# Fillers of 32 and 992 bytes in the place of 64 and 960 around the normalised input: it begins at 160 modulo 2048 in a partition

## What is computed

```python
for l in range(DEPTH):                      # 2
    h = rmsnorm(x, norm_mix[l])
    p = h @ w_in[l]                         # 2048 x 4608
    ...                                     # differential attention (q, k, v), pooling mixer, convolution mixer
    x = x + concat([y_b, y_a, y_c]) @ w_out[l]      # 2048 x 2048
    h = rmsnorm(x, norm_ffn[l])
    gu = h @ w_ffn_in[l]                    # 2048 x 11008
    g = causal_dwconv(gu[..., :D_FF], ffn_conv_w[l], ffn_conv_b[l])
    x = x + (silu(g) * gu[..., D_FF:]) @ w_ffn_out[l]   # 5504 x 2048
return rmsnorm(x, final_norm)
```

## The kernel before, in words

| tile | bytes | begins at, modulo 2048 |
|---|---|---|
| `x` | 16384 | 128 |
| `xg` (and over it, for the end of layer 1, `xt`, `gains`, `ss`, `rt`) | 32768 | 192 |
| `ssq` | 1024 | 192 |
| `raw`, `whi`, `wlo` | 16384 each | 128 |
| `half`, `gt` | 4096, 4128 | 1184 |
| `y` | 4096 | 1216 |
| `hidden1` | 88064 | 128 |
| `mix`, `hidden0`, `qT` | 32768, 88064, 8192 | 192 |
| `pw_sb` | 8192 | 672 |

## Time and profile before

### The profile page before, as it was taken

One profiled execution on the slowest core, in us unless ns is written; L12 is line 12 of the kernel. 1 busy time (PEld: TensorE's weight loads), 2 busy tenths in 40 slices (PEclk: granted clock), 3 DMA queues, 4 the chain that ended last, 5 costly groups with the idle time before them and its releaser, 6 DMA issues.

```text
span 2082.2 us, 32567 instructions
## 1 busy us (share of the span) xinstructions
PE 2065.1 (99%) x11564; PEld 1792.5 (86%) x11564; DVE 1418.0 (68%) x2009; ACT 1081.7 (52%) x1509; POOL 23.5 (1%) x20
## 2 busy tenths in 40 slices
PE   9999999999999999999999999999999999999998
PEld 8888888888888888888888888888888888888886
DVE  7998777676666665555489978676666666654454
ACT  6556655555555554433374566455555555544444
POOL 0001100000000000000000011000000000000000
PEclk9999999999999999999999999999999999999999
DMA  8554354555555555555565444555555555555554
GB/s 290 176 186 158 129 191 178 206 188 191 189 189 185 198 192 190 195 194 180 207 209 198 176 147 137 198 191 190 191 190 181 200 186 195 185 212 192 194 200 162
DMA packets 108943, 392.66 MB, mean 189 GB/s; under 512 B 12224, under 2 KB 12736, under 8 KB 108480
## 3 DMA queue, kind: packets, MB, share of 16 engines
q1 hardware_dynamic: 106992, 386.45, 53.8%
q10 hardware_dynamic: 1872, 5.13, 0.7%
HBM read 389.43 MB, written 2.10 MB: 188 GB/s over the span
## 4 chain that ended last, share of the span: by engine, by line
PE 96%; DVE 2%; ACT 1%; DMA 0%; issue 0%; ACTq 0%; DVEq 0%
PE bank L1177 52%; PE bank L1180 26%; PE bank L1452 4%; PE bank L1451 4%; PE bank L1450 4%; PE bank L1264 2%; PE bank L1253 1%; PE bank L1254 1%; PE bank L1255 1%; DVE wlo L734 0%; DMA x<-xT 0%; PE bank L1315 0%; ACT whi L404 0%; DVE y L806 0%; PE bank L1425 0%; ACT E L500 0%
## 5 line engine op out<-in xcount | busy, mean ns | idle before, releaser
L734 DVE TENSOR_TENSOR wlo<-raw,whi 128x1024 fp32r<-128x1024 f32 x728 | 886.4, 1223 | 609.6 <-ACT whi L404 608.9
L1177 PE MATMUL bank<-xg,whi 128*128 128x512 f32 x3648 | 1135.5, 393 | 2.5 <-DVE wlo L714 2.5
L404 ACT ACTIVATE whi<-raw 128x1024 fp32r<-128x1024 f32 x728 | 764.2, 1057 | 692.9 <-PE bank L1180 556.1
L1180 PEld LDWEIGHTS bank<-xg,wlo 128*128 128x128 f32 x3648 | 685.0, 188 | 151.2
L1180 PE MATMUL bank<-xg,wlo 128*128 128x256 f32 x3648 | 720.0, 279 | 0.0
L1177 PEld LDWEIGHTS bank<-xg,whi 128*128 128x128 f32 x3648 | 552.9, 188 | 6.9 <-issue 3.3
L1177 PE MATMUL bank<-hidden,whi 128*128 128x512 f32 x688 | 213.5, 392 | 0.0
L1177 PE MATMUL bank<-mix,whi 128*128 128x512 f32 x512 | 160.8, 395 | 0.5 <-DVE mix L878 0.5
L1180 PEld LDWEIGHTS bank<-hidden,wlo 128*128 128x128 f32 x688 | 129.2, 188 | 28.5
L1180 PE MATMUL bank<-hidden,wlo 128*128 128x256 f32 x688 | 135.9, 279 | 0.0
L1450 PE MATMUL bank<-whi,hidden 128*128 128x512 f32 x344 | 134.6, 391 | 0.0
(11 more groups left out here) (150 smaller groups left out, 1142.7 us busy)
## 6 DMA issues: line engine op xcount, KB each, us to landing
raw<-wstream SPq DMA_DIRECT2D x729, 512.0 KB, 3.3
pw_sb<-pww ACTq DMA_DIRECT2D x2, 1024.0 KB, 7.4
outT<-xt SPq DMA_DIRECT2D x8, 256.0 KB, 2.9
x<-xT SPq DMA_DIRECT2D x2, 512.0 KB, 10.2
gains<-gain_rows ACTq DMA_DIRECT2D x1, 1024.0 KB, 5.6
raw<-wstream SPq DMA_DIRECT2D x2, 256.0 KB, 4.1
x<-xT ACTq DMA_DIRECT2D x2, 256.0 KB, 5.4
x<-xT SPq DMA_DIRECT2D x2, 256.0 KB, 7.2
```

Of the source, the lines that this page charges most:

```text
L404: nc.scalar.activation(whi[:, s, :], raw[:, s, :], ACT.Copy).then_inc(hi_ready, 1)
L734: nc.vector.tensor_tensor(wlo[:, s, :], raw[:, s, :], whi[:, s, :], ALU.subtract).then_inc(lo_ready, 1)
L1177: nc.tensor.matmul(ps[bank][:], whi[:, s, blk * P:blk * P + P], mov, start=first, stop=False)
L1180: return nc.tensor.matmul(ps[bank][:, 0:S], wlo[:, s, blk * P:blk * P + P], mov[:, 0:S], start=False, stop=last)
```

## The change

The filler ahead of `xg` shrinks from 16 to 8 numbers of 4 bytes, and the one behind `ssq` grows from 240 to 248. So `xg`, what lies over it (`xt`, `gains`, `ss`, `rt`) and `ssq` begin 32 bytes earlier in every partition: `xg`, `xt`, `gains` and `ssq` at 160 modulo 2048 in the place of 192. All other tiles stay where they were. No instruction is added, removed or moved on any engine.

```diff
         x = sb("x", [P, KC, S])
-        sb("offset0", [P, 16])
+        sb("offset0", [P, 8])
         with ExitStack() as until_ffn_out:
             xg = sb("xg", [P, KC, 2 * S], f32r, until_ffn_out)
         xt = sb("xt", [P, 2, DM])
...
         sb("rest", [P, KC * 2 * S - 3 * DM - 16])
         ssq = sb("ssq", [P, S])
-        sb("offset1", [P, 240])
+        sb("offset1", [P, 248])
         raw = sb("raw", [P, RING, PIECE])
```

## The result

The changed kernel takes 2089.61 us (median of 8 runs, 2089.18 to 2090.34) against 2083.78 us of the kernel before (8 runs, 2083.23 to 2084.34): 5.83 us more, a ratio of 1.0028 with a 95% interval of 1.0019 to 1.0037. The forecast was 2088.4 us, with 2085.5 to 2091.5 for its likeliest case.

A forecast was written before the change was run, and what follows sets the result against it. PE's matmul stream, busy 99% of the span, was taken to bound the kernel; +6.1 us for group on xg and -1.3 us for the value parts made +4.8 on 2083.57, so 2088.4 us, range 2072 to 2112 us.

The forecast's parts named there:

- What bounds the kernel: Whole kernel: PE is busy 99% and hardly waits, so time follows the distance between matmuls; excess is stalls of 16 columns.
- Term 1: group on xg, 912 rounds of eight matmuls: 16 stalls in place of 15, +6.1 us, bounds -69 to +54.7.
- Term 2: Value parts, 384 matmuls with xg stationary: midway between 3 and 2 stalls, -1.3 us, bounds 0 and -2.6.
- Terms 3 and 4: Elementwise work on xg, xt, gains, ssq, and transfers such as stores from xt: 0 each, plus or minus 0.3 us.
- Term 5: Tiles that stay (mix, hidden0, hidden1, weights): output projection and FFN's second product cost what they did, 0.
- No change: Rival for the matmuls on xg: 15 stalls stay 15, time 2083.6 us, or 2082.3 with the value parts' gain; chance 0.28.
- A half line on every matmul: Rival: each moving operand straddles 64-byte lines at both ends, +24.3 us (2107.9) or +48.6 us (2132.2); chance 0.21.
- Faster: Rival: load and stream pass between lines, a round of eight loses stalls, 2077.5 or 2071.4 us, at lowest 2014; chance 0.18.

The follow-up runs named there:

- 352: xg moved alone to 352 by changing only the two fillers, against the kernel before: +22.4 us.
- the low half alone: wlo alone moved up by 64 bytes to 192, whi and raw staying at 128, against the kernel before: 2110.88 us against 2083.61, ratio 1.0131.

## Why the prediction was right

**What bounds the kernel** held: PE's stream and nothing else. The reading of the excess as whole stalls of 16 columns held too: the counts of the loop, 2031, 2021, 2012, 2003 and 1993, lie 9 or 10 apart, with only 352 (1995) and the low half alone (2007) between two steps; in the value part a distance of 64 gives 2.3 a matmul, which is 7 in three. What the excess was put down to, one meeting of load and stream for each stall, is not shown, and the low half alone speaks against it in that simple form.

**Term 1, group on xg, +6.1 us:** right, 16 stalls for 15, 912 times. The FFN loop's stretch of 455.50 us now holds 2629 starts in the place of 2643, so what was there takes 457.9 us, beside 457.7 foretold. But part of the reason was wrong. I placed the new distance between two known ones, the 15 stalls of 64 and the 16 of distance 0, and took the latter from the token group. `group` itself has 17 at distance 0, so 16 is the middle of a straight line 17, 16, 15, and not the end of it. The token group's rate could not be carried over: it streams 512 columns each time and has another order of loads. The neighbour on the other side, 96 bytes, has 18, and no interpolation from the trace of before would have given that. That the number came out right is partly luck: the change moved towards the side on which a reference, if a poor one, existed, and that reference was one stall too low.

**Term 2, the value parts, -1.3 us:** wrong; it is 0, and the step did not fall towards 230 ns as foretold. After the change the timeline of the value part has 22 steps in 5.14 us, as before in 5.13:

```profile
69.67 0.40 PE L1254 MATMUL bank<-wlo,xg 128*128 128x512 f32 x1
...
74.81 0.40 PE L1255 MATMUL bank<-whi,xg 128*128 128x512 f32 x1
```

The middle between 3 and 2 stalls was taken where there is a step: at -32 bytes it still has 3, at 0 it has 2. With 0 in its place the sum is +6.1, beside 5.83 measured; with the -1.3 it was +4.8, so the forecast was one microsecond short.

**Terms 3 and 4,** elementwise work and stores at 32 modulo 64: 0, as said. The tiles of the earlier trace rows did not move; on those that did, ScalarE's mean for `xg<-x,par` is 497 ns against 495, VectorE's 481 as before, none of the others on `xt`, `gains` and `ssq` differs by more than 3 ns, and `outT<-xt` lands in 2.8 us against 2.9. **Term 5,** the tiles that stay: 0, their counts are the same within one.

**The rivals.** *No change* fell with the count of 2021 and an interval clear of 1. The rule of the Trainium skill beside it (TensorE: Matmul & The Clock Gate, Part 2), that loading the next weights steals nothing from the running matmul, does not hold here as a rule on time: moving the weights by 32 bytes took the stretch on `hidden0`, which stayed, from 15 to 16 stalls. Whether what is lost is read bandwidth is not shown. *A half line on every matmul* fell at this distance (+24 us was its price); prices of that size do exist at 96, 160 and 224, whether by this mechanism or another is open. *Faster* fell: of the eight distances modulo 256 in steps of 32 none has fewer than 15 stalls, and the kernel before sits on the lowest.

## What to carry to other kernels

When PE never waits and yet takes longer than its columns, compare the distances between starts of streams of the same form whose tiles begin at different addresses; counting the starts in a stretch of fixed length resolves a tenth of a per cent. In such a kernel a tile's address is a parameter, and it counts against the tile on the other side of the same matmul: moving the weights changes every stream that uses them, so the price of a shift has to be summed over all of them. Don't interpolate between places that have not been measured in the same form of stream; here, from the best distance of 64 bytes, a step of 32 costs one stall a round on one side and three on the other.

## What the runs showed that was not expected

- In these streams, where each matmul has its own load of 128 float32 columns, the excess over the columns is 13 to 21 ns for 512 columns with the granted clock at 1.00 (2.4 GHz), and depends on the distance modulo 256 bytes between the beginnings of the moving and the stationary operand. The best and the worst of the eight distances are 15 and 19 stalls of 16 columns in a round of eight, 23.6 us or 1.1% of this kernel.
- The best distance depends on the form of the stream: 64 for `group` (15; 17 at 0), 0 for the value part (2.0 a matmul; by its own distance 2.3 at 64, 2.9 to 3.2 elsewhere). The token group was measured at 0 and 32 only (2 and 3).
- What exactly meets what is open. The runs show that it takes both addresses, and that the stalls of neighbouring matmuls hang together (the low half alone). A step smaller than 32 bytes was not tried, and neither was a stream without loads beside it.
